# Feed-forward products of a two-block transformer: from split hi/lo products to plain 32-bit ones with stationary weights, fed by one ring of 1 MB tiles

## The chip, the cores and the metric

The kernel runs on one core of one Trainium2 chip. The metric is the device time of one execution in microseconds (us). A core has five engines: TensorE (PE in the profile, with its weight loads listed apart as PEld), VectorE (DVE), ScalarE (ACT), GpSimd (POOL) and SyncE (SP). DMA transfers are issued from the engines' queues (SPq, ACTq).

## The reference

256 positions of width 1024 pass through two blocks. Everything is 32-bit floating point.

```python
def swiglu(h, wg, wu, wd):
    return (jax.nn.silu(h @ wg) * (h @ wu)) @ wd

# first block, two layers
for l in range(DEPTH):
    h = rms_norm(x, norm1_g[l]); p = h @ w_in[l]              # 1024 x 1792
    ya, yb, yc = pool_mixer(...), gmlp_mixer(...), conv_module(...)
    x = x + jnp.concatenate([ya, yb, yc], axis=-1) @ w_out[l]
    h = rms_norm(x, norm2_g[l])
    x = x + (swiglu(h, ffn_wg, ffn_wu, ffn_wd)                # l == 0, d_ff 2816
             if l == 0 else moe_swiglu(h, ...))               # l == 1, top 2 of 8, d_ff 3584
# second block, two layers
    h = x @ w_in_2[l]                                         # 1024 x 1704
    mix = concat(sliding-window attention, sparse attention) @ w_o_2[l]
    x = layer_norm(ALPHA * x + mix)
    ffn = (silu(x @ w_gate) * (x @ w_up)) @ w_down            # d_ff 2816
    x = layer_norm(ALPHA * x + ffn + (p @ w_pp) * sigmoid(x @ w_pg))
```

So there are three dense feed-forward layers of inner width 2816 for all 256 tokens, and one mixture of eight experts of inner width 3584. The kernel gives each expert a block of 128 places for its tokens.

## The kernel before

The program is one straight sequence of stages: mixer 0, dense feed-forward 0, mixer 1, routing, eight experts, attention 0, dense feed-forward 1, attention 1, dense feed-forward 2, last layer norm, store. Each engine has its own instruction stream. Semaphores tie the streams together.

**The feed-forward stages** run in steps of 256 inner columns (`FN`): 11 steps for a dense one (`STEPS`), 14 for an expert (`STEPS_E`), so 33 and 112 steps. A step does this:

- SP loads 1 MB of gate columns and 1 MB of up columns into one of the two slots of `ringA`, and 1 MB of down rows into one of the two slots of `ringD` (`gate_up` L354 and L355, `rows` L359).
- ACT rounds each half of the weights to a short "hi" part (`split_up` L981, `split_down` L991); DVE subtracts it from the weights to get the "lo" part (L1323, L1329). The tokens are split in the same way (`split_stream` L1016 and L1357, or L1040 and L1499 for an expert's tokens).
- PE multiplies in three products: token-hi by weight-hi, token-hi by weight-lo, token-lo by weight-hi (`parts`, L522 to L524). The tokens are the stationary operand, 128 of them at a time, and 512 weight columns (256 gate and 256 up) are the moving one. An expert step has 24 such products for gate and up and 12 for down; a dense step has twice as many.
- ACT takes `silu` of the gate (L974), DVE multiplies (L1317), PE transposes the result (`turn_act`, by way of L481) and ACT and DVE split it again (L996, L1333), before PE can do the down product.

```python
mm(out, x0, w0[:, wide], start=start, stop=False)
mm(out, x0, w1[:, wide], start=False, stop=False)
return mm(out, x1, w0[:, wide], start=False, stop=stop)
```

The `mm` operands are, in order, the output in PSUM, the stationary operand, and the moving operand. The split parts have the type `float32r`. All other products of the kernel, such as `project` (L503), `full_depth` (L513), `gather` (L692) and `scatter` (L708), are plain 32-bit ones. Each of them appears in the trace as two records, each with its own weight load, which is why their counts are twice those of the code. Each `float32r` product is one record.

**Around the experts**, PE gathers an expert's tokens with 16 plain products of 128 by 128 by 128 (`gather`), and puts the result back with four plain products of 512 columns (`scatter`). The gate factors are transposed with two transposes (`turn_gates`). ACT moves the expert's result out of PSUM first (L1046), and DVE adds the scattered rows to `X` (L1506).

**Between stages**: `to_features` (L481) transposes the 256 tokens; ACT and DVE copy the transposes to `hT` (L969, L1309, L1311). In the second block, `full_depth` of `w_pg_2` comes just ahead of the feed-forward; ACT then takes its sigmoid (L1258). DVE closes a dense stage by adding the down product to `X` (`add_down`, L1375). SP loads are issued in the order of use; each waits until the slot's earlier content was used. Loops are hardware loops (`Fori`).

The functions that the change touches are printed here.

Of the kernel before, what the change touches and what calls it, by code (L numbers as in the profile page):

```python
# [9 lines left out]
P128 = 128  # L10
# [29 lines left out]
FN = 256  # L40
STEPS, STEPS_E = D_FF // FN, D_FF_E // FN
MOE_STEP0 = STEPS
B2_STEP0 = MOE_STEP0 + EXPERTS * STEPS_E
TOP_E = 2

# [29 lines left out]
def build_program(nc, T):  # L75
# [6 lines left out]
    with ctx:  # L82
# [7 lines left out]
        def sb_rounded(name, shape):  # L90

            start = -(-nc.sbuf_base // 32) * 32
            wide = sb(name, shape)
            return wide, nc.alloc_sbuf_tensor_at(name + "_rounded", shape, f32r, offset=start)

# [14 lines left out]
        lnp = sb("lnp", [128, DEPTH, 4, D])  # L110
        lni = sb("lni", [128, 3, D])
        X = sb("X", [128, NB, D])
        hT, hTr = sb_rounded("hT", [128, KT, SEQ])
        XN, XNr = sb_rounded("XN", [128, NB, D])
        ringA = sb("ringA", [128, 2, 4096])
        ringD = sb("ringD", [128, 2, 2048])
        sil = sb("sil", [128, 2, NB, FN])
        am = sb("am", [128, 2, NB, FN])
        aT = sb("aT", [128, 2, 2, SEQ], f32r)
# [8 lines left out]
        SCR, SCRr = sb_rounded("SCR", [128, 16600])  # L128
# [37 lines left out]
        def scr_r(n):  # L166
            at[0] += n
            return SCRr[:, at[0] - n:at[0]]

# [23 lines left out]
        UH, UL = [None, None], [None, None]  # L193
        for h in range(2):
            UH[h], UL[h] = scr_r(2048), scr_r(2048)
        DH, DL = scr_r(2048), scr_r(2048)
        XGH, XGL = (scr_r(KT * P128).rearrange("p (k n) -> p k n", k=KT) for _ in range(2))
        aTl = scr_r(2 * 2 * SEQ).rearrange("p (c f n) -> p c f n", c=2, f=2)

        xh = XNr[:, :, :].rearrange("p b n -> p (b n)").rearrange("p (k n) -> p k n", k=KT)  # L200
        xl = hTr[:, :, :]

        at[0] = 0
# [4 lines left out]
        OT = scr(2 * P128).rearrange("p (f n) -> p f n", f=2)  # L208

# [43 lines left out]
        A_loaded = [sem("A_loaded0"), sem("A_loaded1")]  # L253
        D_loaded = [sem("D_loaded0"), sem("D_loaded1")]
# [23 lines left out]
        gu_psum, silu_ready, act_ready, aT_psum, aT_ready, down_done, ffn_evac = (  # L278
            sem(n) for n in ("gu_psum", "silu_ready", "act_ready", "aT_psum", "aT_ready", "down_done", "ffn_evac"))
        u_hi, u_ready = [sem("u_hi0"), sem("u_hi1")], [sem("u_ready0"), sem("u_ready1")]  # L280
        u0_used, d_hi, d_ready, aT_hi, xs_hi, xs_ready, xg_hi = (
            sem(n) for n in ("u0_used", "d_hi", "d_ready", "aT_hi", "xs_hi", "xs_ready", "xg_hi"))
# [55 lines left out]

        block = ctx.enter_context(nc.Block())
# [3 lines left out]
        def _(sp):  # L343
            def cut(w, e, r0, rows, c0, n):

                return w[bass.ds(e, 1), bass.ds(r0, rows), bass.ds(c0, n)].rearrange("o (k p) n -> p (o k) n", p=128)

            def columns(slot, w, e, c0, n):
                dst = ringA[:, slot, 0:KT * n].rearrange("p (k n) -> p k n", k=KT)
                sp.dma_start(dst, cut(w, e, 0, D, c0, n)).then_inc(A_loaded[slot], 32)  # L350

            def gate_up(slot, wg, wu, e, cg, cu):
                dst = ringA[:, slot, :].rearrange("p (k u n) -> p k u n", k=KT, u=2)
                sp.dma_start(dst[:, :, 0, :], cut(wg, e, 0, D, cg, FN)).then_inc(A_loaded[slot], 16)  # L354
                sp.dma_start(dst[:, :, 1, :], cut(wu, e, 0, D, cu, FN)).then_inc(A_loaded[slot], 16)  # L355

            def rows(slot, w, e, r0):
                dst = ringD[:, slot, :].rearrange("p (k n) -> p k n", k=2)
                sp.dma_start(dst, cut(w, e, r0, FN, 0, D)).then_inc(D_loaded[slot], 16)  # L359

            def step_weights(wg, wu, wd, e, up0, s0, y, j):

                sp.wait_ge(u_ready[1], s0 + y - 1)
                gate_up(j, wg, wu, e, y * FN, y * FN + up0)
                down_rows(wd, e, s0, y - 2, (j + 1) % 2)

            def down_rows(wd, e, s0, y, slot):
                wait(sp, d_ready, s0 + y - 1)
                rows(slot, wd, e, y * FN)

            def feed_forward(wg, wu, wd, e, up0, s0, n):

                gate_up(1, wg, wu, e, FN, up0 + FN)
                step_weights(wg, wu, wd, e, up0, s0, 2, 0)
                step_weights(wg, wu, wd, e, up0, s0, 3, 1)
                with sp.Fori(2, n // 2) as i:
                    for j in range(2):
                        step_weights(wg, wu, wd, e, up0, s0, 2 * i + j, j)
                if n % 2:
                    step_weights(wg, wu, wd, e, up0, s0, n - 1, 0)  # L380
                down_rows(wd, e, s0, n - 2, (n - 1) % 2)
                down_rows(wd, e, s0, n - 1, n % 2)

            def load(dst, src, s):
                sp.dma_start(dst, src).then_inc(s, 16)

# [7 lines left out]
            load(par[R_GMB:ROWS, 0:128], T["gm_b"].rearrange("l h i -> (l h) i"), par_loaded)  # L394
            for l in range(DEPTH):
                for c in range(4):
                    if c >= 2:
                        sp.wait_ge(proj_psum, 4 * l + c - 1)
                    elif l:
                        sp.wait_ge(u_ready[1], STEPS)  # L400
                    columns(c % 2, T["w_in"], l, D_IN - C1 * (c + 1), C1)
                if l:
                    sp.wait_ge(d_ready, STEPS)
                sp.dma_start(ringD[:, 0, 0:3 * D_CONV].rearrange("p (k n) -> p k n", k=3),
                             cut(T["conv_pw_w"], l, 0, D_CONV, 0, D_CONV)).then_inc(D_loaded[0], 16)
                for n in range(2):
                    sp.wait_ge(proj_psum, 4 * l + n + 3)
                    columns(n, T["w_out"], l, 512 * n, 512)
                if l == 0:
                    sp.wait_ge(mix_psum, 1)  # L410
                    gate_up(0, T["ffn_wg"], T["ffn_wu"], 0, 0, 0)
                    sp.wait_ge(mix_psum, 2)
                    feed_forward(T["ffn_wg"], T["ffn_wu"], T["ffn_wd"], 0, 0, 0, STEPS)

            EG, EU, ED = T["moe_wg"], T["moe_wu"], T["moe_wd"]
            sp.wait_ge(mix_psum, 3)
            gate_up(0, EG, EU, 0, 0, 0)
            sp.wait_ge(mix_psum, 4)
            gate_up(1, EG, EU, 0, FN, FN)

            def further_steps(e, s0):
                with sp.Fori(0, STEPS_E // 2 - 1) as i:
# [24 lines left out]
            with sp.Fori(0, DEPTH) as l:  # L447
# [3 lines left out]
                for c in range(4):  # L451
                    if c >= 2:
                        sp.wait_ge(proj_psum, 4 * q + c - 1)
# [1336 lines left out]
```

## Time and profile before

| | |
|---|---|
| median of 3 runs | 2409.42 us (2408.99 to 2409.75) |
| span of the profiled execution | 2408.6 us, 0.8 us under that median |
| mean granted TensorE clock | 0.937 of full speed |
| PE / PEld busy | 2142.4 us (89%) / 1613.2 us (67%) |
| DVE / ACT / POOL busy | 1454.0 (60%) / 1113.6 (46%) / 75.8 us (3%) |
| DMA | 525.73 MB, 218 GB/s on average |

The span runs from the first to the last instruction of the profiled execution. No time of that execution beside its span is recorded, so the difference of 0.8 us is taken between the span and the median of the timed runs. Matmuls are pipelined: a record's duration is longer than the distance to the next record, and it is the distance ("pitch") that adds up. The granted clock is given as a share of the full 2.4 GHz; a stretch at 0.5 would be at the lower level of 1.2 GHz throughout.

### The profile page before, as it was taken

Reading aid. Unit: us, or ns where it says so; the run is one execution under the profiler, and the core shown is the slowest. Engines: PE = TensorE matmul, PEld = TensorE weight load, DVE = VectorE, ACT = ScalarE, POOL = GpSimd, SP = SyncE. Lnnn points to the kernel's source line nnn. Section 1 sums busy time; section 2 is a strip of 40 time slices with the busy share of each in tenths; the row PEclk is TensorE's granted clock in tenths of the full one; section 3 lists DMA queues with packets and bytes.
Section 4 is the critical chain, followed back from the end, with each engine's and each line's share of the span. In section 5 each row is a group of like instructions: output and inputs, shape, how many; then the busy total and the mean of one; then the engine's idle time right before and its main releaser. Section 6 shows DMA issues by size and latency. Waiting matters only on the chain.

```text
span 2408.6 us, 25214 instructions
## 1 busy us (share of the span) xinstructions
PE 2142.4 (89%) x8930; PEld 1613.2 (67%) x8931; DVE 1454.0 (60%) x1519; ACT 1113.6 (46%) x1120; POOL 75.8 (3%) x28
## 2 busy tenths in 40 slices
PE   7569998569999999999999999785989988688997
PEld 4247874257888787878787878644557874555885
DVE  0634442537888888888888888645245443623544
ACT  2134432126767676767767676503134330313332
POOL 0400000300000000000000000010000001000000
PEclk9789998779999999999999999986799999689999
DMA  5345432138989899999999999630145523014541
GB/s 187 121 175 210 174 131 106 47 122 309 371 319 371 322 372 341 352 344 349 363 328 366 326 365 350 241 115 36 42 151 212 207 94 139 11 70 172 211 158 53
DMA packets 378875, 525.73 MB, mean 218 GB/s; under 512 B 10360, under 2 KB 326344, under 8 KB 378828
## 3 DMA queue, kind: packets, MB, share of 16 engines
q1 hardware_dynamic: 372700, 515.99, 59.5%
q10 hardware_dynamic: 6128, 9.08, 1.0%
q8 instruction: 33, 0.54, 0.1%
q14 instruction: 14, 0.11, 0.0%
HBM read 523.99 MB, written 1.05 MB: 218 GB/s over the span
## 4 chain that ended last, share of the span: by engine, by line
PE 82%; DVE 7%; ACT 4%; issue 3%; POOL 2%; DMA 1%; DVEq 0%; ACTq 0%; SPq 0%
PE ps L522 19%; PE ps L523 19%; PE ps L524 19%; PE ps L503 8%; PE ps L513 7%; PE ps L481 4%; POOL SCR L912 2%; PE ps L692 1%; PE ps L708 1%; ACT SCR_rounded L981 1%; DMA ringA<-in_w_gu 1%; PE ps L855 1%; DVE SCR_rounded L1323 1%; PE ps L883 1%; PE ps L658 1%
## 5 line engine op out<-in xcount | busy, mean ns | idle before, releaser
L1323 DVE TENSOR_TENSOR SCR_rounded<-ringA,SCR_rounded 128x2048 fp32r<-128x2048 f32 x290 | 664.5, 2293 | 288.8 <-ACT SCR_rounded L981 288.0
L981 ACT ACTIVATE SCR_rounded<-ringA 128x2048 fp32r<-128x2048 f32 x290 | 556.2, 1919 | 269.1 <-PE ps L524 211.8
L524 PE MATMUL ps<-SCR_rounded 128*128 128x512 f32 x1608 | 630.6, 392 | 0.0
L1329 DVE TENSOR_TENSOR SCR_rounded<-ringD,SCR_rounded 128x2048 fp32r<-128x2048 f32 x145 | 332.3, 2292 | 102.6 <-ACT SCR_rounded L991 102.6
L522 PE MATMUL ps<-SCR_rounded 128*128 128x512 f32 x896 | 350.7, 391 | 9.5 <-DVE SCR_rounded L1333 4.6
L991 ACT ACTIVATE SCR_rounded<-ringD 128x2048 fp32r<-128x2048 f32 x145 | 278.5, 1921 | 161.4 <-PE ps L524 161.1
L523 PE MATMUL ps<-SCR_rounded 128*128 128x512 f32 x896 | 348.8, 389 | 0.0
L524 PEld LDWEIGHTS ps<-SCR_rounded 128*128 128x128 f32 x1608 | 302.0, 188 | 67.4
L522 PE MATMUL ps<-SCR_rounded,aT 128*128 128x512 f32 x712 | 296.0, 416 | 2.0 <-DVE SCR_rounded L1329 2.0
L523 PE MATMUL ps<-SCR_rounded,aT 128*128 128x512 f32 x712 | 282.2, 396 | 0.0
L522 PE MATMUL ps<-SCR_rounded,XN_rounded 128*128 128x512 f32 x528 | 210.0, 398 | 19.2 <-DVE hT_rounded L1357 7.0
L523 PE MATMUL ps<-SCR_rounded,XN_rounded 128*128 128x512 f32 x528 | 209.0, 396 | 0.0
L524 PE MATMUL ps<-SCR_rounded,hT_rounded 128*128 128x512 f32 x528 | 209.0, 396 | 0.0
L522 PEld LDWEIGHTS ps<-SCR_rounded 128*128 128x128 f32 x896 | 168.2, 188 | 49.1 <-issue 5.8
L503 PE MATMUL ps<-ringA,hT 128*128 128x448 f32 (+1 forms) x512 | 195.3, 543 | 3.8 <-DVE hT L1311 1.9
L523 PEld LDWEIGHTS ps<-SCR_rounded 128*128 128x128 f32 x896 | 168.2, 188 | 34.7
L974 ACT ACTIVATE sil<-ps 128x256 f32<-128x256 f32 (+1 forms) x145 | 62.8, 433 | 226.6 <-PE ps L524 226.6
L503 PEld LDWEIGHTS ps<-ringA,hT 128*128 128x128 f32 x512 | 99.3, 195 | 96.7 <-issue 94.0
L481 PE MATMUL ps<-ident,SCR 128*128 128x128 f32 (+1 forms) x248 | 52.1, 390 | 122.5 <-POOL SCR L912 47.5
L522 PEld LDWEIGHTS ps<-SCR_rounded,aT 128*128 128x128 f32 x712 | 133.9, 188 | 30.7 <-issue 4.3
L523 PEld LDWEIGHTS ps<-SCR_rounded,aT 128*128 128x128 f32 x712 | 134.8, 189 | 27.7 <-issue 1.7
L481 PEld LDWEIGHTS ps<-ident,SCR 128*128 128x128 f32 (+1 forms) x248 | 44.3, 206 | 130.9 <-POOL SCR L912 48.3
(228 smaller groups left out, 1854.4 us busy)
## 6 DMA issues: line engine op xcount, KB each, us to landing
ringA<-in_moe_wg SPq DMA_DIRECT2D x112, 1024.0 KB
ringA<-in_moe_wu SPq DMA_DIRECT2D x112, 1024.0 KB
ringD<-in_moe_wd SPq DMA_DIRECT2D x112, 1024.0 KB, 7.5
ringA<-in_w_gu SPq DMA_DIRECT2D x44, 1024.0 KB
ringD<-in_w_down SPq DMA_DIRECT2D x22, 1024.0 KB, 5.8
ringA<-in_w_in SPq DMA_DIRECT2D x8, 1792.0 KB
ringA<-in_w_in SPq DMA_DIRECT2D x8, 1704.0 KB
ringA<-in_ffn_wg SPq DMA_DIRECT2D x11, 1024.0 KB
```

The costliest lines, as they stand in the source:

```text
L481: return nc.tensor.transpose(out, in_, ident[0:n, 0:n])
L503: m = mm(ps[:, 4 + 2 * (c % 2) + b, 0:n], hT[:, k, b * 128:(b + 1) * 128], w[:, k, :], start=(k == 0), stop=(k == KT - 1))
L513: m = mm(ps[:, bank_of(b), :], lhs[:, k, b * 128:(b + 1) * 128], w[:, k, :], start=(k == 0), stop=(k == KT - 1))
L522: mm(out, x0, w0[:, wide], start=start, stop=False)
L523: mm(out, x0, w1[:, wide], start=False, stop=False)
L524: return mm(out, x1, w0[:, wide], start=False, stop=stop)
L912: TTn(YB, YB, Pm[:, :, U0:U0 + D_GM], ALU.mult).then_inc(yb_ready, 1)
L974: fn(sil[:, par_, 0:blocks, :], ps[:, 2 * par_:2 * par_ + blocks, 0:FN], ACT.Silu).then_inc(silu_ready, 1)
L981: fn(UH[h], ringA[:, par_, 2048 * h:2048 * h + 2048], ACT.Copy).then_inc(u_hi[h], 1)
L991: fn(DH if unit is None else UH[unit], ringD[:, slot, :], ACT.Copy).then_inc(d_hi, 1)
L1323: V.tensor_tensor(UL[h], ringA[:, par_, 2048 * h:2048 * h + 2048], UH[h].bitcast(f32), ALU.subtract).then_inc(u_ready[h], 1)
L1329: V.tensor_tensor(lo, ringD[:, (par_ + 1) % 2, :], hi.bitcast(f32), ALU.subtract).then_inc(d_ready, 1)
```

## The change

1. **Plain products.** The splits of weights and tokens, `split_up`, `split_down`, `split_act`, `split_stream` and `parts` go, and so does `turn_act`. Gate, up and down products are plain 32-bit ones.
2. **Operands swapped for gate and up.** The stationary operand is a 128 by 128 piece of the weights, and the moving one is the tokens (128 for an expert, 256 for a dense stage). The result is already transposed, with inner columns on the partitions, and becomes the stationary operand of the down product, whose moving operand is 512 columns of the down weights.
3. **Order.** Work goes in chunks of 128 inner columns (22 for a dense stage, 28 for an expert), in groups of four: gate of group s, down of group s-1, up of group s.
4. **One ring** of eight 1 MB tiles for every weight of the program. SP's loads are in order of use; each waits only for the last use of the tile eight places before. A tile has 2 KB or 4 KB runs (1 KB in the last, two-chunk group of a dense stage), where `gate_up` had 1 KB runs.
5. **Straight code.** The `Fori` loops over steps, experts and the second block's layers are unrolled. PE no longer takes part in the branch for experts with more than 128 tokens; the other engines keep it. In the recorded execution no instruction of that branch ran.
6. Smaller: the scatter is done in two halves, one group apart, except behind the last expert; the layer-norm rows are loaded one layer at a time (two pairs of loads move behind `features` on ACT's queue); the two `conv_pw_w` loads come together at the start into a buffer of their own.

```diff
-            def parts(out, wide, x, w, start, stop):
...
+            def up_phase(i0, n, t, x, toks, col0, bank_left, back, done):
+
+                per = 4 if n == 4 else KT
+                for c in range(n):
+                    if i0 + c >= back:
+                        pe.wait_ge(bank_left, i0 + c + 1 - back)
+                    for k in range(KT):
+                        if c == 0 and k % per == 0:
+                            arrived(t + k // per)
+                        m = mm(ps[:, (i0 + c) % 4, col0:col0 + toks], slot(t + k // per, per)[:, k % per, c * 128:c * 128 + 128],
+                               x[:, k, :], start=(k == 0), stop=(k == KT - 1))
                     m.then_inc(done, 1)
...
+            def gate_phase(i0, n, t, x, toks):
+                up_phase(i0, n, t, x, toks, 0, act_ready, 4, g_psum)
+
+            def upward_phase(i0, n, t, x, toks):
+                up_phase(i0, n, t, x, toks, toks, silu_ready, 0, u_psum)
+
+            def down_phase(i0, n, t, blocks, first, last):
+                for c in range(n):
+                    pe.wait_ge(act_ready, i0 + c + 1)
+                    if c % 2 == 0:
+                        arrived(t + c // 2)
                     for b in range(blocks):
...
+                        for h in range(2):
+                            m = mm(ps[:, 4 + 2 * b + h, :], aT[:, (i0 + c) % 4, b * 128:(b + 1) * 128],
+                                   slot(t + c // 2, 2)[:, c % 2, 512 * h:512 * h + 512],
+                                   start=(first and c == 0), stop=(last and c == n - 1))
+                    if c % 2:
+                        m.then_inc(down_tiles, 1)
...
+                for s, n in enumerate(FF_GROUPS):
+                    gate_phase(i, n, gate[s], hT, SEQ)
+                    if s:
+                        if s == 1 and before_down:
+                            pe.wait_ge(sgp_ready, before_down)
+                        down_phase(i - 4, 4, down[s - 1], NB, s == 1, False)
+                    upward_phase(i, n, upward[s], hT, SEQ)
+                    i += n
+                down_phase(i - n, n, down[end], NB, False, True)
...
+            gate, upward, down = FF_MOE
+            i, s = FF_CHUNKS, 0
+            for e in range(EXPERTS):
+                x = XG[e % 2]
+                for j in range(MOE_GROUPS[e]):
+                    if j == 0:
+                        pe.wait_ge(xg_ready, e + 1)
+                    gate_phase(i, 4, gate[s], x, P128)
+                    if e and j in (1, 2):
...
+                        scatter(j - 1, (6, 7), scat_psum)
+                    if s:
+                        down_phase(i - 4, 4, down[s - 1], 1, j == 1, j == 0)
+                    upward_phase(i, 4, upward[s], x, P128)
+                    if j == 3:
...
+                        turn_gates(PG, 6, gt_psum)
+                    if j == 4 and e + 1 < EXPERTS:
+                        pe.wait_ge(gt_ready, e + 1)
+                        gather(lambda b: PL[:, b, e + 1, :], xg_psum)
+                    i, s = i + 4, s + 1
+            down_phase(i - 4, 4, down[s - 1], 1, False, True)
```

```diff
+            def fetch(t, src, k, n):
+                if t >= SLOTS:
+                    name, count = ends[t - SLOTS]
+                    sp.wait_ge(counted[name], count)
+                sp.dma_start(ring[:, t % SLOTS, 0:k * n].rearrange("p (k n) -> p k n", k=k),
+                             src.rearrange("(k p) n -> p k n", p=128)).then_inc(tile_loaded[t % SLOTS], 16)
...
+            def silu(i, toks):
+                act.wait_ge(g_psum, i + 1)
+                if i >= 4:
+                    act.wait_ge(act_ready, i - 3)
+                fn(sil[:, i % 4, 0:toks], ps[:, i % 4, 0:toks], ACT.Silu).then_inc(silu_ready, 1)
...
+            def act_mul(i, toks):
+                dve.wait_ge(silu_ready, i + 1)
+                dve.wait_ge(u_psum, i + 1)
+                V.tensor_tensor(aT[:, i % 4, 0:toks], sil[:, i % 4, 0:toks], ps[:, i % 4, toks:2 * toks],
                                 ALU.mult).then_inc(act_ready, 1)
```

## Rows read from the trace of the kernel before

**Rows 1.** The page's busy times, and its chain that ended last by engine.

```profile
PE 2142.4 (89%) x8930; PEld 1613.2 (67%) x8931; DVE 1454.0 (60%) x1519; ACT 1113.6 (46%) x1120; POOL 75.8 (3%) x28
...
PE 82%; DVE 7%; ACT 4%; issue 3%; POOL 2%; DMA 1%; DVEq 0%; ACTq 0%; SPq 0%
```

**Rows 2.** Four stretches: length, busy per engine, granted clock, DMA share, GB/s.

```profile
162.40:360.66 198.26, 191.58 (x836) 154.78 (x836) 89.10 (x59) 73.54 (x57) 0.00 (x0) 0.98 0.48 172
536.60:1556.00 1019.40, 1007.88 (x4560) 814.49 (x4560) 868.59 (x626) 718.59 (x589) 0.00 (x0) 1.00 0.95 342
1784.70:1980.20 195.50, 189.85 (x836) 153.19 (x836) 92.98 (x60) 74.44 (x56) 0.00 (x0) 1.00 0.52 185
2197.40:2393.30 195.90, 189.82 (x837) 153.25 (x836) 93.41 (x60) 74.43 (x56) 0.00 (x0) 1.00 0.47 166
```

**Rows 3.** Timeline of an expert on PE: start, us, instruction, operands.

```profile
824.27 3.74 PE L692 MATMUL ps<-hT,XN 128*128 x32
...
827.77 0.48 PE L522 MATMUL ps<-SCR_rounded 128*128 128x512 f32 x1
...
828.08 0.40 PE L523 MATMUL ps<-SCR_rounded 128*128 128x512 f32 x1
...
833.09 0.40 PE L524 MATMUL ps<-SCR_rounded 128*128 128x512 f32 x1
```

**Rows 4.** Timeline, weight loads of plain products with 512, then 426 moving columns.

```profile
1757.46 0.19 PEld L513 LDWEIGHTS ps<-ringA,hT 128*128 128x128 f32 x1 [0.24 <-issue]
...
1783.64 0.19 PEld L513 LDWEIGHTS ps<-ringA,hT 128*128 128x128 f32 x1 [0.24 <-issue]
...
1996.17 0.19 PEld L503 LDWEIGHTS ps<-ringA,hT 128*128 128x128 f32 x1 [0.17 <-issue]
...
1999.74 0.19 PEld L503 LDWEIGHTS ps<-ringA,hT 128*128 128x128 f32 x1 [0.17 <-issue]
```

**Rows 5.** Timeline, first products of expert 0 and last scatter.

```profile
535.38 1.08 ACT L1040 ACTIVATE SCR_rounded<-ps 128x512 fp32r<-128x512 f32 x2 [10.53 <-PE ps L692]
...
537.36 0.50 PE L522 MATMUL ps<-SCR_rounded 128*128 128x512 f32 x1 [2.01 <-DVE SCR_rounded L1499]
...
1551.09 1.02 ACT L1046 ACTIVATE band<-ps 128x1024 f32<-128x1024 f32 x1 [5.54 <-PE ps L524]
1552.26 3.67 PE L708 MATMUL ps<-band 128*128 128x512 f32 x8 [1.21 <-ACT band L1046]
1555.96 2.48 DVE L1506 TENSOR_TENSOR X<-X,ps 128x512 f32<-128x512 f32 x4 [8.09 <-PE ps L708]
```

**Rows 6.** Timeline, from the end of the first dense feed-forward to the next projection.

```profile
360.66 2.35 DVE L1375 TENSOR_TENSOR X<-X,ps 128x1024 f32<-128x1024 f32 x2 [6.47 <-PE ps L524]
...
368.62 3.67 PE L481 MATMUL ps<-ident,XN 128*128 128x128 f32 x16 [8.00 <-DVE XN L1301]
373.27 3.36 PE L503 MATMUL ps<-ringA,hT 128*128 128x448 f32 x4 [0.97 <-DVE hT L1311]
```

**Rows 7.** Timeline, from the token transposes into the first dense feed-forward.

```profile
157.76 3.67 PE L481 MATMUL ps<-ident,XN 128*128 128x128 f32 x16 [6.93 <-DVE XN L1301]
...
167.47 0.77 PE L522 MATMUL ps<-SCR_rounded,XN_rounded 128*128 128x512 f32 x1 [6.03 <-issue]
...
171.45 0.56 PE L522 MATMUL ps<-SCR_rounded,XN_rounded 128*128 128x512 f32 x1
```

**Rows 8.** Timeline, token transposes and first product of routing.

```profile
509.28 3.67 PE L481 MATMUL ps<-ident,XN 128*128 128x128 f32 x16 [6.93 <-DVE XN L1301]
...
515.46 6.04 PE L674 MATMUL ps<-router,hT 128*128 128x8 f32 x32 [2.50 <-DVE hT L1311]
```

**Rows 9.** Timeline, both ends of the second dense feed-forward.

```profile
1784.69 1.88 ACT L1258 ACTIVATE SCR<-ps 128x2048 f32<-128x2048 f32 x1 [0.55 <-PE ps L513]
...
1980.17 2.35 DVE L1375 TENSOR_TENSOR X<-X,ps 128x1024 f32<-128x1024 f32 x2 [6.47 <-PE ps L524]
```

**Rows 10.** DMA view of the stretch 700 to 1500 us.

```profile
DMA packets 208724, 278.66 MB, mean 348 GB/s; under 512 B 4240, under 2 KB 186192, under 8 KB 208720
```

More of the change, by code:

```diff
@@ L343, in _ @@
         def _(sp):
[L344 to L369, printed above, removed]
@@ new lines, in columns, with rows, up_columns, feed_weights @@
+            def columns(t, w, c0, n):
+                for h in range(2):
+                    fetch(t + h, w[512 * h:512 * h + 512, c0:c0 + n], 4, n)
+            def rows(t, w, r0, n):
+                for j in range(n):
+                    fetch(t + j, w[r0 + 256 * j:r0 + 256 * j + 256, :], 2, D)
+            def up_columns(t, w, c0, n):
+                if n == 4:
+                    columns(t, w, c0, 512)
+                else:
+                    fetch(t, w[:, c0:c0 + 256], KT, 256)
+            def feed_weights(tiles, groups, source):
+                gate, upward, down = tiles
+                for s, n in enumerate(groups):
+                    wg, wu, wd, c0, u0 = source(s)
+                    up_columns(gate[s], wg, c0, n)
+                    if s:
+                        _, _, wd_, r0, _ = source(s - 1)
+                        rows(down[s - 1], wd_, r0, groups[s - 1] // 2)
+                    up_columns(upward[s], wu, c0 + u0, n)
+                rows(down[-1], wd, c0, groups[-1] // 2)
@@ L751, in _, with scatter @@
+            def scatter(b, banks, done):
+                for n in range(2):
+                    m = mm(ps[:, banks[n], :], GT[:, b * 128:(b + 1) * 128], YE[:, n * 512:(n + 1) * 512],
+                           start=True, stop=True)
+                m.then_inc(done, 1)
             pe.wait_ge(xn_gained, 1)
             pe.wait_ge(pl_ready, 1)
-            gather(places_of(0), xg_psum)
-            expert(0, MOE_STEP0, first=True)
-            with pe.Fori(1, EXPERTS - 1) as e:
-                expert(e, MOE_STEP0 + STEPS_E * e)
@@ L917, in _ @@
             pool.wait_ge(rope_tables, 8)
-            with pool.Fori(0, DEPTH) as l:
+            for l in range(DEPTH):
                 def heads(c0, n, d):
@@ L1186, in _ @@
             tokens_out(0)
-            expert(0, MOE_STEP0, first=True)
-            with act.Fori(1, EXPERTS - 1) as e:
-                expert(e, MOE_STEP0 + STEPS_E * e)
-            expert(EXPERTS - 1, B2_STEP0 - STEPS_E, last=True)
-            split_act(B2_STEP0 - 1, 1, 1)
-            split_down(B2_STEP0 - 1, 1, 63, unit=1)
-            output_out(B2_STEP0)
+            i = FF_CHUNKS
+            for e in range(EXPERTS):
+                for j in range(MOE_GROUPS[e]):
+                    for c in range(4):
+                        silu(i + c, P128)
+                    i += 4
+                    if j == 0 and e:
+                        output_out(e - 1)
+                    if j == 3:
+                        gates_out(e)
+                    if j == 4 and e + 1 < EXPERTS:
+                        tokens_out(e + 1)
+            output_out(EXPERTS - 1)
             def second_block(r, e):
```

670 lines of the change are left out of this document (221 added, 449 removed).

## The prediction

> **What bounds the kernel now.** I read the busy times and the chain that ended last first [rows 1]. The reader should see that PE is busy 89% of the span and makes 82% of the chain, so time is PE's time almost everywhere. Then I cut out the four feed-forward stretches, because only they change their arithmetic [rows 2]. PE is busy 99% of the experts' stretch and 97% of each dense one, at a granted clock of 1.00 (0.98 in the first). These four add to 1609 us, two thirds of the span. DMA moves 342 GB/s in the experts' stretch at a share of 0.95, so there the weights are a near second; in the dense stretches they are not. DVE and ACT have slack in all four. So the question is only: how many us of PE time does the new arithmetic take, and which gaps at the stages' ends does it close?
>
> The experts' stretch is 1019.4 us long, some 127 us for each of the eight.
>
> **Prices of a product.** The new products are not new to the trace.
> - Plain, 128 by 128 stationary, 128 moving columns: that is the gather. From its first record to the next product is 827.77 - 824.27 = 3.50 us for 16 products [rows 3], so 0.219 us each.
> - Plain, 512 moving columns: the first and the last of 62 evenly spaced weight loads stand 26.18 us apart [rows 4]. That is 0.429 us a record and 0.858 us a product.
> - Plain, 426 columns: 11 loads over 3.57 us [rows 4], 0.714 us a product.
> - Plain, 256 columns: the trace has no steady run of it at the full clock. The straight line from 128 to 512 columns gives 0.715 for 426, which is what was measured, so I take the line: 0.432 us. Both sides are close: the cost per column of the 512-column product gives 0.429, that of the 128-column product 0.438.
> - Before, a split product of 512 columns: (833.09 - 828.08) / 22 = 0.228 us [rows 3].
>
> A plain product of 512 columns thus costs 3.77 split ones, and the split scheme used three. That is the heart of the forecast. Swapping the operands changes nothing in it: the same columns times rows times depth pass the array, in narrower products that have almost the same price per column.
>
> **The change part by part.**
>
> *A chunk of 128 inner columns.* An expert's chunk has 8 gate and 8 up products of 128 columns, 16 x 0.219 = 3.50 us, and 2 down products of 512, 1.72 us: 5.22 us. A dense chunk has 16 products of 256 columns, 6.91 us, and 4 of 512, 3.43 us: 10.34 us.
>
> *Experts.* 8 x 28 chunks x 5.22 = 1169.3 us. Inside them lie 7 gathers (24.5 us), 7 scatters of four 512-column products (24.0 us) and 8 pairs of gate transposes (about 2 us), none of it new. Together 1219.8 us. The start: before, ACT and DVE split the gathered tokens, and PE began at 537.36 [rows 5]. Now one ACT copy of 128x1024 does it. The like copy at 1551.09 took 1.02 us and PE went on 1.17 us after its start, so PE begins at about 535.38 + 1.1 = 536.5. The last product ends near 1756.3; the copy out and its wait take 1.4 us, as before. So the last scatter starts at 1757.7 in place of 1552.26: +205.4. Of the four adds behind it (2.48 us) two now lie beside the second half's products: -1.2.
>
> *Ahead of routing and ahead of the first dense stage*, DVE no longer splits weights before it copies the transposes. Where nothing is split, the first product starts 373.27 - 368.62 = 4.65 us after the transposes do [rows 6]. Ahead of the first dense stage it is 167.47 - 157.76 = 9.71 us, with the token splits in it [rows 7]. Ahead of routing it is 515.46 - 509.28 = 6.18 us [rows 8], so 1.5 us go there: -1.5. Experts in all: 205.4 - 1.2 - 1.5 = +202.7.
>
> *First dense stage.* Start 157.76 + 4.65 = 162.4; 22 x 10.34 = 227.6 us; and 2.0 us for a start at the lower clock. Before, that lasted from 167.47 to 171.45 [rows 7], at pitches about twice the later ones, so half of 4 us was lost. End and last drain: 392.3, against 360.66 [rows 6]: +31.6.
>
> *Second and third dense stages.* Before, `w_pg_2` ended at 1784.69 and the down product was added at 1980.17 [rows 9], 195.5 us; the third has the same length within 0.4 us [rows 2]. In this time PE also waited for the token splits and for gate weights, since SP could refill a `ringA` slot only after it was used. With the ring, the first tiles of the stage replace those of `w_o_2` and land during the `w_pg_2` products, and nothing stands between them and the first gate product. Stage: 227.6 + 0.2 = 227.8 us, +32.3 and +32.0.
>
> *The sum*: 31.6 + 202.7 + 32.3 + 32.0 = +298.6 us on a span of 2408.6, so 2707.2; with the 0.8 us by which the median lies above the span, 2708.0.
>
> *What I cost at nothing, and what covers it.* The silu and multiply of a chunk: ACT and DVE are less loaded than before, and between the up product of a chunk and the down product that needs it lies a whole gate phase (7.0 us for experts, 13.8 for dense groups), save at a stage's last group, where PE still has the down product of the chunk before (3.4 us dense). Without this cover each group would wait under 1 us. The weights: a group of four expert chunks uses six tiles, 6.29 MB, in 20.9 us, which is 301 GB/s; before, 348 GB/s were moved over 800 us [rows 10], with shorter runs. A tile's place is asked for again some 20 us ahead of need. Behind a late tile on SP's queue stand all later ones, the attention's too, but the queue holds eight. The layer-norm loads on ACT's queue stand ahead of the projections' copies, for which a whole projection of products is still to run. The early loads compete at the start with the mixer's, half a stage before use. Not joining the overflow branch frees PE where it waited for DVE anyway. Everything in mixers and attention is otherwise the same.
>
> *Bounds.* Waits stand before every gate, up and down chunk, 870 in all. A satisfied wait costs nothing visible in the middle of that run, but the first product after a change of kind comes 0.31 - 0.228 = 0.08 us late [rows 3]. If each wait cost that: +70, so 2778. From below: the products' clock alone, four clocks of 2.4 GHz a column (512 columns, 0.853 us), without the few ns on top, over 3584 products of 128, 1056 of 256 and 744 of 512 columns in the four stretches saves 30 us, and no slow start another 2: 2676.
>
> **The rivals.**
>
> *The clock falls.* The expert products are narrow and broken by a wait in each chunk. If a quarter of the experts' time ran at 1.2 GHz, it would take 0.25 x 1220 = 305 us more: 3013. For it: after the pause ahead of the first dense stage the clock was low for 4 us [rows 7]. Against it: the gathers in the middle of the experts are the same narrow stream, and the whole stretch has 1.00 [rows 2]. It needs PE to run idle, so a late tile or token. 5%. The Trainium skill ("TensorE: Matmul & The Clock Gate", HAM oscillation) tells of a product with few rows that fell to the low clock again and again, because each short burst of products was followed by a longer wait for data; by that rule this change is dangerous where a tile comes late.
>
> *Weight loads come into the open.* Each record has a load of its own, 0.19 us long [rows 4]. If they no longer hid behind products, 10704 records x 0.19 = 2034 us would be added: 4740. The gather speaks against it, with load and product together in 0.109 us a record. 1%. The Trainium skill (same page, What overlaps and what doesn't) states that loads overlap running products only if their row groups differ; the gather's pitch in this trace disagrees.
>
> *The weights bound the experts.* It decides below 301 GB/s. At 280 GB/s a group takes 22.5 us, 56 groups 90 us more: 2797. 4%.
>
> *The straight code is not fetched in time.* The nearest row is the chain's 3% "issue", 72 us [rows 1]; twice as much gives 2780. 5%.
>
> *Not slower: the narrow product is cheaper than the gather says.* If the gather's 0.109 us a record were its weight load and not its columns, and the load were shared by both records in the new stream, a 128-column product could cost half: 3584 x 0.109 = 391 us less, 2317. It decides at 0.219 - 298.6 / 3584 = 0.136 us a product. Against it: 128, 426 and 512 columns lie on one line that leaves only 0.006 us for no columns at all, so the columns set the price at 128 too. 2%, and 1% for something between that ends within 0.2%, which is about what a measurement can tell from no change.
>
> **How the numbers follow.** The forecast, all prices as above, has the remaining 82%. It gives 2708. Its own bounds, 2676 and 2778, are ends that need every product or every wait to be off in one way. The range reaches a little past the upper one, to take in the fetch and part of the DMA case: 2680 to 2785. Faster 2%, same 1%, slower 97%.
>
> **What the profile of the changed kernel would show.** Experts: gathers 28 x 5.22 + 3.5 + 3.4 + 0.3 = 153.4 us apart, gate and up records 0.109 us apart, down records 0.429. Dense: group after group 41.4 us apart; records of 256 columns 0.216 apart. DMA near 300 GB/s in the experts, DVE and ACT under 20% busy there. First gate product of the later dense stages right behind the last of `w_pg_2`. The forecast is wrong if PE shows idle time inside a stage, a clock below 1.00 there, or other pitches.

## The result, and the profile after

The changed kernel takes 2715.76 us (median of 4 runs, 2715.15 to 2716.66); the kernel before took 2409.2 us beside it. The ratio is 1.1276, with a 95% interval of 1.126 to 1.1292: 12.8% slower. The profiled execution took 2716.66 us with a span of 2714.8 us, 306.2 us more than the span before.

The page of the changed kernel: busy times, the chain by engine, then the three costliest groups of products, one load of weights from section 5 and the queue of instructions from section 3.

```profile
PE 2479.6 (91%) x12870; PEld 1844.1 (68%) x12870; DVE 416.6 (15%) x1055; ACT 272.0 (10%) x671; POOL 75.2 (3%) x28
...
PE 89%; DVE 5%; ACT 2%; POOL 2%; issue 1%; DMA 0%; ACTq 0%; DVEq 0%
...
L542 PE MATMUL ps<-SCR,ring 128*128 128x128 f32 x7168 | 812.0, 275 | 1.1 <-ACT SCR L950 1.1
L559 PE MATMUL ps<-ring,aT 128*128 128x512 f32 x1424 | 623.3, 592 | 0.0
L542 PE MATMUL ps<-hT,ring 128*128 128x256 f32 x2112 | 458.9, 379 | 1.0 <-DVE hT L1210 1.0
...
L542 PEld LDWEIGHTS ps<-SCR,ring 128*128 128x128 f32 x7168 | 810.3, 192 | 27.6 <-issue 26.3
...
q8 instruction: 102, 1.67, 0.2%
```

Against [rows 1] the reader sees the trade plainly. DVE fell from 1454 to 417 us and ACT from 1114 to 272 us, and neither was on the path. PE rose by 337 us, and PE is the path: 89% of the chain. The feed-forward products themselves wait for 2.1 us in the whole program. The instruction queue fetched more for the straight code, 1.67 MB in place of 0.54, and that is not seen as a wait: "issue" is 1% of the chain, where it was 3%.

The same four stretches as in [rows 2], by the windows view (length, busy time of PE, PEld, DVE, ACT, POOL, granted clock, DMA share, GB/s):

```profile
161.40:389.20 227.80, 227.75 (x880) 167.12 (x880) 9.27 (x23) 8.70 (x23) 0.00 (x0) 1.00 0.42 144
563.00:1804.00 1241.00, 1239.43 (x8368) 1009.16 (x8367) 86.03 (x271) 81.57 (x248) 0.00 (x0) 1.00 0.77 284
2028.50:2256.00 227.50, 227.50 (x881) 166.91 (x879) 13.90 (x25) 12.91 (x25) 0.00 (x0) 1.00 0.44 150
2472.20:2700.00 227.80, 227.54 (x881) 166.91 (x879) 14.13 (x26) 12.89 (x25) 0.00 (x0) 1.00 0.35 122
```

PE has next to no gap in any of them (1.6 us in the 1241), the clock is at its full 2.4 GHz throughout, and the weights come at 284 GB/s with a DMA share of 0.77. So the whole length of a stretch is its number of products times their price. The prices stand in the chain of the changed kernel (start, us, what, records). L542 is gate and up, L559 the down product, L687 the gather:

```profile
216.85 27.63 PE ps L542 x128
...
796.32 7.15 PE ps L542 x64
803.46 6.87 PE ps L559 x16
810.33 7.14 PE ps L542 x64
817.48 3.57 PE ps L687 x32
821.05 7.15 PE ps L542 x64
828.20 6.87 PE ps L559 x16
835.07 14.29 PE ps L542 x128
849.36 6.87 PE ps L559 x16
856.23 3.79 PE ps L542 x34
...
990.41 4.69 PE ps L542 x42
```

A product is two records. 128 columns: 14.29 / 64 = 0.2233 us. 512 columns: 6.87 / 8 = 0.859 us. 256 columns, from the dense stage: 27.63 / 64 = 0.4317 us. One expert follows the other after 990.41 - 835.07 = 155.34 us, where 153.4 was forecast; a dense group is 27.63 + 13.73 = 41.4 us, as forecast.

Where the 306.2 us lie is read from the same mark in each trace, the first product of a projection. The column "plain products alone" belongs to the first experiment, which has only the plain products and nothing else of the change.

| from, to | before | plain products alone | whole change |
|---|---|---|---|
| start to first block's second projection | 373.27 | +41.4 | +28.5 |
| to second block's first projection (mixer, routing, experts) | 1207.5 | +218.7 | +218.3 |
| to second block's second projection (attention, dense) | 414.9 | +39.5 | +28.7 |
| to the end (attention, dense) | 412.9 | +40.8 | +30.7 |
| span | 2408.6 | +340.4 | +306.2 |

Attention in the third stretch is 2.9 us shorter than before; 2.0 us of that lie in its first projection, which ran at a mean granted clock of 1.00 in place of 0.96 (46.07 in place of 48.10 us). The dense stage in it is 31.6 us longer.

### The profile page after: what moved, and what is told of

It is laid out like the page before. It is cut to its first block, busy times and chain, and to the rows that moved or that the text cites. A ratio compares the mean times of both kernels' runs of the same rounds, so it can differ in the third digit from the quotient of the medians.

```text
span 2714.8 us, 29533 instructions
## 1 busy us (share of the span) xinstructions
PE 2479.6 (91%) x12870; PEld 1844.1 (68%) x12870; DVE 416.6 (15%) x1055; ACT 272.0 (10%) x671; POOL 75.2 (3%) x28
## 3 DMA queue, kind: packets, MB, share of 16 engines
q8 instruction: 102, 1.67, 0.2%
## 4 chain that ended last, share of the span: by engine, by line
PE 89%; DVE 5%; ACT 2%; POOL 2%; issue 1%; DMA 0%; ACTq 0%; DVEq 0%
PE ps L542 46%; PE ps L559 23%; PE ps L515 7%; PE ps L526 6%; PE ps L491 2%; POOL SCR L882 2%; PE ps L687 1%; PE ps L699 1%; PE ps L827 1%; ACT SCR L1133 1%; PE ps L854 1%; PE ps L652 1%; DVE SCR L1519 1%; DVE SCR L1540 0%; ACT XN L930 0%
## 5 line engine op out<-in xcount | busy, mean ns | idle before, releaser
L542 PEld LDWEIGHTS ps<-SCR,ring 128*128 128x128 f32 x7168 | 810.3, 192 | 27.6 <-issue 26.3
L542 PE MATMUL ps<-SCR,ring 128*128 128x128 f32 x7168 | 812.0, 275 | 1.1 <-ACT SCR L950 1.1
L559 PE MATMUL ps<-ring,aT 128*128 128x512 f32 x1424 | 623.3, 592 | 0.0
L559 PEld LDWEIGHTS ps<-ring,aT 128*128 128x128 f32 x1424 | 267.4, 190 | 312.8 <-issue 311.9
L542 PE MATMUL ps<-hT,ring 128*128 128x256 f32 x2112 | 458.9, 379 | 1.0 <-DVE hT L1210 1.0
L542 PEld LDWEIGHTS ps<-hT,ring 128*128 128x128 f32 x2112 | 401.2, 190 | 63.1 <-issue 8.1
L1216 DVE TENSOR_TENSOR aT<-sil,ps 128x128 f32<-128x128 f32 (+1 forms) x290 | 92.3, 318 | 1772.9 <-PE ps L542 1772.9
L515 PE MATMUL ps<-ring,hT 128*128 128x448 f32 (+1 forms) x512 | 193.1, 539 | 3.9 <-DVE hT L1210 1.9
L515 PEld LDWEIGHTS ps<-ring,hT 128*128 128x128 f32 x512 | 98.3, 193 | 95.3 <-issue 90.2
L526 PE MATMUL ps<-ring,SCR 128*128 128x512 f32 x256 | 115.4, 611 | 6.2 <-ACT SCR L1059 2.6
L526 PEld LDWEIGHTS ps<-ring,hT 128*128 128x128 f32 x128 | 24.2, 190 | 32.3 <-issue 29.7
```

Source lines behind the costliest of these rows:

```text
L515: m = mm(ps[:, 4 + 2 * (c % 2) + b, 0:n], hT[:, k, b * 128:(b + 1) * 128], w[:, k % 4, :], start=(k == 0), stop=(k == KT - 1))
L526: m = mm(ps[:, 4 + 2 * b + n, :], lhs[:, k, b * 128:(b + 1) * 128], slot(t + k // 2, 2)[:, k % 2, 512 * n:512 * n + 512], start=(k == 0), ...
L542: m = mm(ps[:, (i0 + c) % 4, col0:col0 + toks], slot(t + k // per, per)[:, k % per, c * 128:c * 128 + 128], x[:, k, :], start=(k == 0), st ...
L559: m = mm(ps[:, 4 + 2 * b + h, :], aT[:, (i0 + c) % 4, b * 128:(b + 1) * 128], slot(t + c // 2, 2)[:, c % 2, 512 * h:512 * h + 512], start= ...
L1216: V.tensor_tensor(aT[:, i % 4, 0:toks], sil[:, i % 4, 0:toks], ps[:, i % 4, toks:2 * toks], ALU.mult).then_inc(act_ready, 1)
```

## The experiments

All medians are beside 2408.15 us (e1 to e4) or 2408.31 us (e5 to e7) for the kernel before.

**Plain products alone.** The kernel before with one plain product for three split ones. The splits still run, and their low parts are not read.

```diff
-                mm(out, x0, w0[:, wide], start=start, stop=False)
-                mm(out, x0, w1[:, wide], start=False, stop=False)
-                return mm(out, x1, w0[:, wide], start=False, stop=stop)
+                return mm(out, x0.bitcast(f32), w0[:, wide].bitcast(f32), start=start, stop=stop)
```

> The kernel before with one plain 32-bit product of the hi parts in place of its three split products; both lo parts are left out of the sum, while ScalarE and VectorE still split everything. Theory (four clocks a column set the time): an expert step has 12 products x 0.858 + 0.2 = 10.5 us, an expert 14 x 10.5 + 7.2 = 154.5 us in place of 126.7 (+222 for eight); a dense stage gains 11 x (24 x 0.858 - 72 x 0.23) = +44 us, three of them +133. Time about 2409 + 355 = 2764 us. Rival (the swap of operands, the ring or the straight code cost the time): no change, about 2409 us, or fewer, since there is a third of the products.

Measured: 2750.75 us, ratio 1.1422 (1.1403 to 1.1441). The theory holds, 13 us too high in sum (a dense stage cost about 40 us more and not 44), and the rival is out. The chain of this kernel in a dense stage, where 48 records are 24 plain products of 512 columns:

```profile
212.73 20.60 PE ps L522 x48
233.77 20.60 PE ps L522 x48
254.81 20.60 PE ps L522 x48
```

20.60 / 24 = 0.858 us a product, where three split ones took 3 x 0.228 = 0.684 us [rows 3]. So the arithmetic alone costs more than the whole change does, +340 us, and the rest of the change gives 34 us back. The table says where: 10 to 13 us in each stretch with a dense stage, 0.4 us in the one with the experts. In a dense stage the 0.44 us of transposes in each step (21.04 us from row to row, less 20.60) and the gaps at its start are gone. In the experts the transposes are gone too, but swapping the operands is dearer there: a group of four chunks has 64 narrow products at 0.2233, 14.29 us, in place of 16 wide ones at 0.858, 13.73 us; 56 groups make that 31 us.

**Half the columns.** The changed kernel, with 64 moving columns in the experts' gate and up products (half of each expert's token places are left out of them).

```diff
-                        m = mm(ps[:, (i0 + c) % 4, col0:col0 + toks], slot(t + k // per, per)[:, k % per, c * 128:c * 128 + 128],
-                               x[:, k, :], start=(k == 0), stop=(k == KT - 1))
+                        cols = 64 if toks == P128 else toks
+                        m = mm(ps[:, (i0 + c) % 4, col0:col0 + cols], slot(t + k // per, per)[:, k % per, c * 128:c * 128 + 128],
+                               x[:, k, 0:cols], start=(k == 0), stop=(k == KT - 1))
```

> The changed kernel with 64 moving token columns in place of 128 in the experts' gate and up products; half of each expert's places are left out. Theory that columns set the price of the narrow product: 3584 products cost half, -400 us, about 2316 us, unless the weights (352 MB at some 370 GB/s, 950 us) bind first: then about 2425. Rival that the load of the weights sets it as much (a load has about the pitch of 128 columns in two passes): the records stay 0.11 us apart and the time stays within 1% of 2716 us.

Measured: 2717.79 us, ratio 1.1287 (1.1268 to 1.1305), the same as with 128 columns, as the rival had it. Its chain in the experts:

```profile
833.64 14.24 PE ps L543 x128
854.79 14.24 PE ps L543 x128
875.96 14.24 PE ps L543 x128
```

Half the columns, and 64 products still take 14.24 us, 0.2225 each. So something that does not depend on the moving columns takes 0.111 us a record, and each record has a load of a fresh 128 by 128 weight tile ahead of it. That the load is this floor is the reading that fits; the runs did not vary the load itself. The Trainium skill ("TensorE: Matmul & The Clock Gate", LDWEIGHTS) gives a load's time in ns as its columns over 1.2, which makes about 107 ns for 128; this pitch of 111 ns is close to that. A load's record is longer than the pitch, 192 ns in the page above, so the loads overlap the products or each other.

**A ring of four tiles** in place of eight (`SLOTS = 4`).

> The changed kernel with a ring of four tiles in place of eight, nothing left out. Theory (products alone set the time, and the ring hides the weights by being asked 20 us ahead): with four tiles a phase's two tiles are asked for when the phase two before it ends, one phase of 7.0 us ahead; two tiles need about 5.7 us at 370 GB/s and 2 us to land the first, so each of the 168 expert phases waits some 0.5 to 1.5 us: +80 to +250 us, 2800 to 2970, more if the clock falls in the waits. Rival (weights are hidden whatever the depth): within 0.5% of 2716 us.

Measured: 2722.04 us, ratio 1.1299 (1.128 to 1.1317). The theory's 2800 us and more did not come; the rival's bound, 0.5%, holds. The interval overlaps that of the ring of eight, but all four times (2718.66 to 2722.61) lie above all four of that kernel (2715.15 to 2716.66), so some 6 us are likely real. PE's busy time in the experts, its only waits for weights in the feed-forward products (us in all, times, longest), and from the page the median time from issue to landing of a tile:

```profile
563.00:1806.00 1243.00, 1240.93 (x8361) 1010.02 (x8360) 85.49 (x270) 80.87 (x248) 0.00 (x0) 1.00 0.77 284
...
PE ps L542 <- DMA ring<-in_moe_wu: 0.4, 1, 0.4
PE ps L542 <- DMA ring<-in_moe_wg: 0.4, 1, 0.4
...
ring<-in_moe_wg SPq DMA_DIRECT2D x112, 1024.0 KB, 6.7
```

PE hardly waits in it. From their first product to their last the experts take 1239.8 us in place of 1236.0, and the second block's two first projections ran at a mean granted clock of 0.95 in place of 1.00 (48.4 us in place of 46.1). The prediction leaned on a tile's place being asked for some 20 us ahead of need; a third of that lead is still nearly cover enough. My price for the smaller ring was far too high: I took 7.7 us from the asking to the landing of a phase's two tiles against 7.0 us of cover, and charged each of 168 phases for it. A tile landed 5.8 to 6.8 us after its issue (the medians of gate, up and down tiles), and the second of the two is not needed at the phase's start.

**Three float32r products in the new order**, from a fixed rounded tile, to see what the split would cost with stationary weights.

```diff
-                        m = mm(ps[:, (i0 + c) % 4, col0:col0 + toks], slot(t + k // per, per)[:, k % per, c * 128:c * 128 + 128],
-                               x[:, k, :], start=(k == 0), stop=(k == KT - 1))
+                        for r in range(3):
+                            m = mm(ps[:, (i0 + c) % 4, col0:col0 + toks], fixed[:, c * 128:c * 128 + 128],
+                                   fixed[:, 0:toks], start=(k == 0 and r == 0), stop=(k == KT - 1 and r == 2))
...
```

The down product is tripled in the same way, with `fixed[:, :]` as its moving operand.

> The changed kernel with three float32r products in place of each plain one in the feed-forward stages, all of them from one fixed tile instead of the weights and tokens (weights are still loaded, but left out of the result): the price of the split scheme with stationary weights. Theory with a weight load of 0.11 us per record as floor: 128 columns 3 x 0.112 = 0.335 us in place of 0.223 (+400 us over 3584 products), 256 columns 3 x 0.115 = 0.345 in place of 0.432 (-92 over 1056), 512 columns 3 x 0.23 = 0.69 in place of 0.858 (-120 over 712): about 2904 us. Rival (one clock a column, loads hidden): 128 columns 3 x 0.056 = 0.17 us (-190): about 2310 us, or what the weights allow.

Measured: 2930.96 us (one run), 27 us above the theory and far from the rival's 2310. Its chain, first a dense stage, then an expert; here a product is one record. The last line is a window in the experts, in the order of the windows above:

```profile
208.29 23.03 PE ps L545 x192
231.32 11.15 PE ps L563 x48
...
923.37 21.39 PE ps L545 x192
...
946.53 5.59 PE ps L563 x24
...
1000.00:1300.00 300.00, 300.00 (x2381) 286.41 (x2380) 15.30 (x50) 15.21 (x46) 0.00 (x0) 1.00 0.61 225
```

float32r at 128 columns: 21.39 / 192 = 0.1114 us. At 256: 23.03 / 192 = 0.120. At 512: 11.15 / 48 = 0.232. Twice the columns from 128 to 256 cost 8% more: at 128 columns the float32r product sits on the same floor of 0.111 us as the plain record. So stationary weights are bad for split products in the experts: three make 0.334 us where before three wide ones, each doing the work of four narrow, made 0.684 / 4 = 0.171. In the dense stages it would nearly break even (3 x 0.120 = 0.360 against 0.342).

**One float32r product**, the same with a single product, so that the weights' arrival is seen when products do not limit.

```diff
+                        for r in range(1):
```

> The changed kernel with one rounded (float32r) product in place of each plain one, both operands from a fixed tile; the weights are still loaded tile by tile and their slots given back in order, but the products do not use them. It leaves the weights out of the feed-forward results. Question: at what rate do the 1 MB tiles arrive when products are not the limit, so how near was the rival 'the weights bound the experts'? PE then needs, by the rows of the run with three such products (0.112 us for 128 columns, 0.120 for 256, 0.230 for 512), 16 x 0.112 + 2 x 0.23 = 2.25 us per expert chunk, 63 us per expert. An expert's 42 tiles are 44 MB. My theory (tiles arrive at the 340 to 365 GB/s that the kernel before moved, so the experts had 15 to 20% to spare): 121 to 130 us between experts, experts' stretch 965 to 1035 us, dense stages 95 to 105 us each; total 2060 to 2150. Rival (the ring's tiles arrive only as fast as the changed kernel was seen to move them, 285 GB/s, so it was near its bound by weights too): 155 us between experts, dense stages 120 us, total above 2450.

Measured: 1876.04 us (two runs), ratio 0.7791 (0.7776 to 0.7805), faster than theory and rival said. Windows of this kernel: in the experts, in the first dense stage, in the second block's attention and projection.

```profile
560.00:1160.00 600.00, 549.83 (x3057) 500.48 (x3057) 58.88 (x186) 57.24 (x174) 0.00 (x0) 0.73 1.04 411
150.00:243.00 93.00, 71.53 (x456) 64.85 (x456) 16.88 (x43) 19.20 (x40) 0.17 (x1) 0.90 0.90 347
1440.00:1540.00 100.00, 91.83 (x424) 62.52 (x423) 20.94 (x35) 15.53 (x27) 0.00 (x0) 0.98 0.75 275
```

The tiles came at 411 GB/s, not at the 348 of the kernel before [rows 10]. A group's 6.29 MB then takes 15.3 us where the products take 21.2, so the changed kernel has 28% to spare on weights. The kernel before had a DMA share of 0.95 at 342 GB/s [rows 2]; this one moves 20% more at a share of 1.04. The tiles' runs are 2 to 4 KB in place of 1 KB, which may be the reason; that alone was not tried. The second thing to see is the clock: 0.73 with PE waiting for tiles again and again (idle 50 of 600 us, no single wait above 1.9 us), against 1.00 in the same code with three products in place of one, where it never waits (the last line of the experiment before).

**Closing the starts of the kernel before.** The 34 us that the rest of the change gave back do not need plain products. Two versions keep the split. The first reorders DVE and gives the tokens' low parts in the second block a place of their own:

```diff
-                for h in range(2):
-                    split_up((0, MOE_STEP0)[l], 0, h)
+                split_up((0, MOE_STEP0)[l], 0, 0)
                 features(2 * l + 1, lambda k: parc[:, k, R_N2 + l:R_N2 + l + 1])
                 if l == 0:
                     split_stream(0)
+                split_up((0, MOE_STEP0)[l], 0, 1)
...
+                split_stream(l + 1, xl2)
                 for h in range(2):
                     split_up(s0, 0, h)
-                dve.wait_ge(pg_psum, 2 * l + 2)
-                split_stream(l + 1)
...
-                sp.wait_ge(sgp_ready, l + 1)
+                sp.wait_ge(pg_psum, 2 * l + 2)
```

> The kernel before, with its three split products kept, and only the stages' starts closed: VectorE copies the transposed tokens and splits them before it splits the second half of the first weights; in the second block the tokens' low parts have a place of their own (over the band matrices, which nothing reads there), so their split does not wait for the last w_pg_2 product; the queue SP asks for the second step's gate weights when the last w_pg_2 product is done, not when the sigmoid is. My theory: PE starts 2.0 us earlier in the first dense stage, 1.5 earlier ahead of routing, and 3.3 earlier in each later dense stage, of which up to 1.5 is given back because the second step's weights still come late: 7 to 10 us less, 2398 to 2401. Rival: what is won at a stage's start is waited for again at its second or third step, since VectorE and ScalarE have the same splits to do and set the pace: 2406 to 2409.

Measured: 2406.22 us, ratio 0.9991 (0.9982 to 1.0). The 7 to 10 us of the theory did not come; the time lies in the rival's range and is not clearly told apart from no change. First product of the second dense stage before, and then in e6 with the first product of its second step, on the timeline:

```profile
1787.97 0.49 PE L522 MATMUL ps<-SCR_rounded,XN_rounded 128*128 128x512 f32 x1 [3.32 <-DVE hT_rounded L1357]
```

```profile
1754.82 27.20 PE L514 MATMUL ps<-ringA,hT 128*128 128x512 f32 x63
1781.46 0.80 PE L523 MATMUL ps<-SCR_rounded,XN_rounded 128*128 128x512 f32 x1
...
1794.60 0.50 PE L523 MATMUL ps<-SCR_rounded,XN_rounded 128*128 128x512 f32 x1 [1.38 <-DVE SCR_rounded L1326]
```

The wait of 3.3 us at the start is gone, and 1.4 us of it comes back one step later, which the theory had allowed for: the second step's weights land late, and their splits with them. The stretch from projection to projection is 412.5 us in place of 414.9. The stretch with the third dense stage gives 0.7 us (412.2 for 412.9): its attention began with a projection at a mean granted clock of 0.96 in place of 1.00, 48.16 us in place of 46.06. The stretch with the experts is 1.3 us longer than before. In the first block a gain of this size can't be read: e6 and the next version, whose code is the same there, reach the second projection at 369.6 and 371.4 us, the kernel before at 373.3.

The second version also puts half of `w_pg_2` into the down slots, so that both gate slots are free when the first half is done:

```diff
-                for n in range(2):
-                    sp.wait_ge(mix_psum, 2 * q + n + 1)
-                    columns(n, T["w_pg_2"], l, 512 * n, 512)
+                sp.wait_ge(mix_psum, 2 * q + 1)
+                columns(0, T["w_pg_2"], l, 0, 512)
+                sp.wait_ge(pp_psum, l + 1)
+                sp.dma_start(ringD[:, :, :].rearrange("p s n -> p (s n)").rearrange("p (k n) -> p k n", k=KT),
+                             cut(T["w_pg_2"], l, 0, D, 512, 512)).then_inc(pg_loaded, 16)
...
+                gate_up(1, T["w_gu_2"], T["w_gu_2"], l, FN, FN + D_FF)
```

> As e6_starts, and besides the second half of w_pg_2 lies in the down weights' two slots (after the w_pp_2 products), so that both gate slots are free as soon as the first w_pg_2 half is done and both first steps' gate weights are asked for then. My theory: the second steps no longer wait: 10 us less than before, 2397 to 2400. Rival (starts are given back later): 2405 to 2409. If e7 equals e6, the second step's weights were in time in e6 too.

Measured: 2401.52 us, ratio 0.9974 (0.9962 to 0.9985): 0.3% faster than the kernel before, and the fastest here that computes everything. It lies between theory and rival: 7 of the theory's 10 us. Both dense stages of the second block gave theirs (411.7 and 409.3 us in place of 414.9 and 412.9). Ahead of the experts the 1.5 us were won and lost again, as these rows of e7 show (L685 the first router product, L703 the gather, then two of the expert's first products), with the same two products in the kernel before below them:

```profile
508.15 3.67 PE L490 MATMUL ps<-ident,XN 128*128 128x128 f32 x16 [6.93 <-DVE XN L1318]
512.79 4.54 PE L685 MATMUL ps<-router,hT 128*128 128x8 f32 x32 [0.97 <-DVE hT L1328]
...
526.64 6.64 PE L703 MATMUL ps<-hT,XN 128*128 128x128 f32 x32 [2.89 <-DVE hT L1496]
...
537.04 0.63 PE L533 MATMUL ps<-SCR_rounded 128*128 128x512 f32 x1
537.46 0.63 PE L531 MATMUL ps<-SCR_rounded 128*128 128x512 f32 x1
```

```profile
537.93 0.39 PE L524 MATMUL ps<-SCR_rounded 128*128 128x512 f32 x1
538.16 0.39 PE L522 MATMUL ps<-SCR_rounded 128*128 128x512 f32 x1
```

Routing starts 4.64 us after the transposes in place of 6.18 [rows 8]. But this gather takes 6.64 us, where it took 5.70 before, and the products behind it start 0.42 us apart for a while, where they started 0.23 apart. It is the clock: over 13.4 us from the gather's start its mean was 0.65 in e7 and 0.85 before. The whole stretch with the experts is 1.1 us longer than before.

## Why the prediction was right, and by how much it was off

Its outcome, 2708.0, lies 7.8 us below the median, inside its range, and its mechanism, plain products that cost more than the splits saved, is what the trace and e1 show. That the sum is off by only half of what the experts' term is off by is luck: the other terms erred the other way. Point by point:

- **A plain product costs 3.77 split ones.** Shown, in the changed kernel (0.432 and 0.859 us for 256 and 512 columns, as predicted) and by itself in e1.
- **The narrow product, 0.219 us.** This is the mis-sized term: it measured 0.2233. I divided the distance from the gather's first record to the *next product* [rows 3], 3.50 us, by 16. The records of that gather stand 0.112 us apart, but the last interval ends after 0.03 us, where the float32r product behind it starts. The chain gives the same gather 3.57 us, and that is the right numerator: 3.57 / 16 = 0.223. 3584 products x 0.0043 = 15.4 us, and the experts' term was off by 218.3 - 202.7 = 15.6 us. The rest of that term held to 0.2 us.
- **The columns set the price at 128 too.** This step was wrong, though its number was not. 128, 256, 426 and 512 columns do lie on one line within 0.01 us, but e2 shows that the line ends at 128: at 64 columns the price stays. The floor and the columns' price nearly meet at that width. "Swapping the operands changes nothing" fell with it by a little: 4% on the experts' gate and up products, 31 us, about half of which my 0.219 already held.
- **The narrow product is cheaper than the gather says** (the case on the other side): its first half, that 0.111 us a record is not the columns' price alone, is borne out; its second, that both records of a product share a load, is not. The trace has a load for every record, 12870 of each.
- **First dense stage, +31.6.** The mark behind it shows +28.5. I had charged 2.0 us for a start at the low clock; the first 192 records took 41.71 us in place of 41.44, so 0.3. The work ahead of the stage ended 1.0 us earlier (transposes at 156.77 in place of 157.76 [rows 7]), which no term held. The other two stages: +31.6 and about +31.4, for +32.3 and +32.0.
- **Satisfied waits cost nothing**: groups follow each other at whole multiples of the product's price. The 70 us of the upper bound were not needed. (The range began at 2680, 4 us above the prediction's own lower bound; nothing hung on it.)
- **The clock falls**: it stayed at 1.00. e5 shows the danger in the same code: once tiles are late, the mean clock is 0.73. The Trainium skill ("TensorE: Matmul & The Clock Gate", HAM oscillation) tells of a clock that falls again and again where each burst of products is followed by a longer wait for data. The clock of e5 falls again and again too, though its waits, at most 1.9 us, are shorter than most of the bursts; the changed kernel has no such waits.
- **Loads in the open**: no; load and product together fit in 0.1117 us a record, though a load's record alone lasts 0.19 us.
- **The weights bound the experts**: no, with more room than I gave. It decides below 6.29 MB / 21.16 us = 297 GB/s, and e5 moved 411.
- **Fetch of straight code**: 1.67 MB on the instruction queue, issue 1% of the chain.

The sum of the errors: experts +15.6, first dense stage -3.1, attention -2.9 and -0.7, the other dense stages -1.3: +7.6 on the span of 2707.2, which is the 2714.8 measured.

## What to carry to other kernels

When a kernel is bound by TensorE, compare arithmetic schemes by the measured pitch per block of work, at the width at which each will run; time freed on DVE and ACT is worth only the gaps that it closes. Take a pitch from equal neighbours, never across a change of instruction. And split a large change at its parts' seams: here the part that lost 340 us hid one that won 34, of which 7 were had with the old arithmetic too.

## What the runs showed of the hardware that was not expected

- In long streams at the full clock, records with a 128 by 128 weight load each came 0.111 to 0.112 us apart, and no closer with fewer columns: plain with 128 or 64 moving columns (0.1117 and 0.1112), float32r with 128 (0.1114). With 256 columns float32r took 0.120, with 512 0.23.
- 1 MB tiles with 2 to 4 KB runs came at 411 GB/s for 600 us on end, where 1 KB runs had given 342 to 348.
- PE that was busy 92% of a stretch, with many waits of at most 1.9 us, had a mean granted clock of 0.73; at 99.9% it had 1.00.
